# Order of splits, turns and taps on three engines, products of constants at the start, and a fourth split buffer for eight tiles, in a two-layer trunk on one core

## The reference

```python
h = rms_norm(x, norm_mix_g[i])
x = x + token_mixing(h, ...)       # w_in, conv, pool, attention, w_branch, gates, w_out
h = rms_norm(x, norm_ffn_g[i])
x = x + (swiglu(h, ...) if i % 2 == 0 else moe_ffn(h, ...))
h = rms_norm(x, norm_ple_g[i])
x = x + sigmoid(h @ ple_w_gate[i]) * (p[i] @ ple_w_proj[i])
# token_mixing, the convolution branch:
v = c_gate * u                     # three taps per channel over v, then
y_conv = b_gate * conv3(v)
```

## Time and profile before

| what | value |
|---|---|
| median of 3 runs | 1243.52 us (1242.11 to 1243.96) |
| profiled execution | 1242.05 us |
| its span, first to last instruction | 1240.3 us |
| mean granted clock of TensorE in it | 0.992 |

### The profile page before, as it was taken

The page is one execution under the profiler, slowest core; times in us unless marked ns, Lnnn a source line. Parts: engine busy times, 40 slices in busy tenths (PEclk is TensorE's granted clock), DMA queues, the critical chain, the costliest instruction groups (busy, mean ns, idle before and its releaser), DMA issues.

```text
span 1240.3 us, 15364 instructions
## 1 busy us (share of the span) xinstructions
PE 1211.2 (98%) x5976; PEld 1008.3 (81%) x5976; DVE 901.6 (73%) x864; ACT 721.5 (58%) x677; POOL 112.7 (9%) x131
## 2 busy tenths in 40 slices
PE   8999999999999999999999999999999999999997
PEld 6887787788888887897778878888888888888876
DVE  6767755654444467657766578898898988888996
ACT  5446544534343456335643467878777777777765
POOL 4700000200000010340000000001000001000301
PEclk9999999999999999999999899999999999999999
DMA  9945454656565555555445489999999999999970
GB/s 294 320 145 195 136 177 162 230 178 200 174 202 175 199 161 186 165 201 170 136 165 174 153 274 376 364 388 375 388 378 387 388 382 385 384 387 379 392 281 35
DMA packets 152204, 317.55 MB, mean 256 GB/s; under 512 B 6273, under 2 KB 41345, under 8 KB 152146
## 3 DMA queue, kind: packets, MB, share of 16 engines
q1 hardware_dynamic: 147328, 302.27, 69.6%
q0 software_dynamic: 4112, 13.44, 3.0%
q10 hardware_dynamic: 706, 1.07, 0.3%
HBM read 310.99 MB, written 5.77 MB: 255 GB/s over the span
## 4 chain that ended last, share of the span: by engine, by line
PE 82%; DVE 9%; ACT 5%; issue 3%; DMA 1%; SPq 0%; POOL 0%; POOLq 0%; ACTq 0%; DVEq 0%
PE ps L1783 22%; PE ps L1528 15%; PE ps L1529 14%; PE ps L1530 14%; PE ps L1770 11%; DVE split L961 3%; ACT split L615 3%; DMA raw<-w_in_dram 1%; PE ps L1750 1%; PE ps L1618 1%; DVE M L1336 1%; DVE hT L993 1%; PE ps L1544 1%; PE ps L1644 1%; PE ps L1739 1%
## 5 line engine op out<-in xcount | busy, mean ns | idle before, releaser
L961 DVE TENSOR_TENSOR split<-raw,split 128x2048 fp32r<-128x2048 f32 x281 | 644.6, 2298 | 242.2 <-ACT split L615 240.0
L615 ACT ACTIVATE split<-raw 128x2048 fp32r<-128x2048 f32 x281 | 538.2, 1916 | 264.2 <-PE ps L1530 190.4
L1783 PE MATMUL ps<-split,br 128*128 128x512 f32 x1344 | 317.5, 392 | 1.5 <-DVE br L1083 1.0
L1783 PEld LDWEIGHTS ps<-split,br 128*128 128x128 f32 x1344 | 249.4, 188 | 56.1 <-issue 2.0
L1528 PE MATMUL ps<-split,hT 128*128 128x512 f32 (+1 forms) x608 | 240.0, 395 | 8.4 <-DVE hT L993 3.3
L1529 PE MATMUL ps<-split,hT 128*128 128x512 f32 (+1 forms) x608 | 234.6, 386 | 0.0
L1530 PE MATMUL ps<-split,hT 128*128 128x512 f32 (+1 forms) x608 | 234.6, 386 | 0.0
L1770 PE MATMUL ps<-split,hT 128*128 128x512 f32 x672 | 159.7, 392 | 0.1
L1770 PEld LDWEIGHTS ps<-split,hT 128*128 128x128 f32 x672 | 124.8, 188 | 28.0 <-issue 1.6
L1528 PEld LDWEIGHTS ps<-split,hT 128*128 128x128 f32 x608 | 115.3, 190 | 36.1 <-DVE hT L993 5.7
L1530 PEld LDWEIGHTS ps<-split,hT 128*128 128x128 f32 x608 | 115.3, 190 | 23.1
(11 more groups left out here) (248 smaller groups left out, 934.7 us busy)
## 6 DMA issues: line engine op xcount, KB each, us to landing
raw<-moe_w_gu_dram SPq DMA_DIRECT2D x96, 1024.0 KB
raw<-moe_w_down_dram SPq DMA_DIRECT2D x56, 1024.0 KB
raw<-w_in_dram SPq DMA_DIRECT2D x45, 1024.0 KB
raw<-ffn_w_gu_dram SPq DMA_DIRECT2D x28, 1024.0 KB
raw<-moe_w_gu_dram SPq DMA_DIRECT2D x32, 512.0 KB
raw<-ffn_w_down_dram SPq DMA_DIRECT2D x14, 1024.0 KB
raw<-w_branch_dram SPq DMA_DIRECT2D x12, 1024.0 KB
raw<-w_out_dram SPq DMA_DIRECT2D x8, 1024.0 KB
```

The source lines that it names most:

```text
L615: act.activation(split[:, t % SPLIT, 0, :], raw[:, t % RAW, :], ACT.Copy).then_inc(hi, 1)
L961: dve.tensor_tensor(split[:, t % SPLIT, 1, :], raw[:, t % RAW, :], split[:, t % SPLIT, 0, :].bitcast(F32), ALU.subtract).then_inc(lo, 1)
L1783: ins = pe.matmul(ps[:, 5 if kind == "up" else 4, :], xe[:, sl, 4 * part + k, :], slot(t, sr, 512)[:, k, :], start=part + k + m == 0, stop ...
```

## The change

It does these things, all in order or place; no computation is left out.
- Constants: TensorE issues 6 products of `ones` by `ones` before it waits for the gain row, and 8 behind the two products that spread it.
- Layer one's tile 4 (second channel tile): its high part stands before the sines on ScalarE, its low part inside `angles()` between the two reductions on VectorE; tile 5's low part takes the former place of tile 4's, ahead of the rotation of k.
- Convolution, both layers: `conv_taps` makes the taps right behind the product C by u (`j in (4, 5)`), the second half into a part of `tmp`; at `j == 7` the split of tile 12 stands behind `conv_y`.
- Between the layers: `turn_lo(3)` stands before the split of u+1; the splits of u+4, u+5 and u+6 stand one place further ahead on both engines; TensorE turns block 1 inside `keys_values` of block 0, behind its sixth of eight steps.
- A fourth split buffer lies in `br` rows 0 to 3 for layer two's tiles 0 and 4, so that for its tiles 0 to 7 the high part waits for the tile four before it.

```diff
@@ -61,6 +61,8 @@
+EXTRA = 8
@@ -212,8 +214,8 @@
             "p (c n) -> p c n", c=CH)
-        cacc = M[:, 0:2, :].rearrange("p b n -> p (b n)")[:, 1536:2048].rearrange(
-            "p (c n) -> p c n", c=2)
+        cacc = [M[:, 0:2, :].rearrange("p b n -> p (b n)")[:, 1536:2048].rearrange("p (c n) -> p c n", c=2),
+                tmp[:, 512:1024].rearrange("p (c n) -> p c n", c=2)]
@@ -302,9 +304,21 @@
+        def buffer(t, s):
...
+            at = t - LAYER_T0[1]
+            if 0 <= at < EXTRA and at % (SPLIT + 1) == 0:
+                return br[:, 2 * s:2 * s + 2, :].rearrange("p r n -> p (r n)")
+            back = 0 if at < 0 else at // (SPLIT + 1) + 1 if at < EXTRA else EXTRA
+            return split[:, (t - back) % SPLIT, s, :]
...
+        def buffers(t):
...
+            return SPLIT + 1 if 0 <= t - LAYER_T0[1] < EXTRA else SPLIT
...
-            return split[:, t % SPLIT, s, :].rearrange("p (k n) -> p k n", n=n)
+            return buffer(t, s).rearrange("p (k n) -> p k n", n=n)
@@ -611,8 +625,8 @@
                 if t >= SPLIT:
-                    act.wait_ge(used, t - SPLIT + 1 + i * per)
-                act.activation(split[:, t % SPLIT, 0, :], raw[:, t % RAW, :], ACT.Copy).then_inc(hi, 1)
+                    act.wait_ge(used, t - buffers(t) + 1 + i * per)
+                act.activation(buffer(t, 0), raw[:, t % RAW, :], ACT.Copy).then_inc(hi, 1)
@@ -796,10 +810,11 @@
                 t0 = LAYER_T0[l]
-                for j in range(l, T_CHAN):
+                for j in range(l, T_CHAN if l else 2):
...
                         p_hi(0, 4)
+                        split_hi(t0 + 4)
@@ -911,6 +926,7 @@
                     p_hi(1, 6)
+                    split_hi(u + 4)
@@ -928,8 +944,6 @@
                             act.activation(sg[:, nh, :], ps[:, 2 * b + nh, :], ACT.Sigmoid).then_inc(psig, 1)
-                    if l == 0 and b:
-                        split_hi(u + 6)
@@ -940,8 +954,8 @@
                         if b == 0:
-                            split_hi(u + 4)
                             split_hi(u + 5)
+                            split_hi(u + 6)
@@ -958,8 +972,8 @@
                 dve.wait_ge(hi, t + 1 + i * per)
-                dve.tensor_tensor(split[:, t % SPLIT, 1, :], raw[:, t % RAW, :],
-                                  split[:, t % SPLIT, 0, :].bitcast(F32), ALU.subtract).then_inc(lo, 1)
+                dve.tensor_tensor(buffer(t, 1), raw[:, t % RAW, :], buffer(t, 0).bitcast(F32), ALU.subtract
+                                  ).then_inc(lo, 1)
@@ -1286,6 +1300,7 @@
                 take_off(4096 * 2 * PI, 7, 6)
+                split_lo(4)
@@ -1296,6 +1311,18 @@
+            def conv_taps(l, half):
...
+                dve.wait_ge(small_in, 48 + 96 * (l + 1))
+                dve.wait_ge(conv_v, 2 * l + half + 1)
+                for c in range(2):
+                    ch, acc = 2 * half + c, cacc[half][:, c, :]
+                    chain(dve.tensor_scalar(acc, vpad[:, ch, 0:SEQ], convw_sb[:, ch, 0:1], None, ALU.mult))
+                    for k in (1, 2):
+                        chain(dve.scalar_tensor_tensor(out=acc, in0=vpad[:, ch, k:k + SEQ],
+                                                       scalar=convw_sb[:, ch, k:k + 1], in1=acc,
+                                                       op0=ALU.mult, op1=ALU.add))
@@ -1310,7 +1337,7 @@
                            4 * l + b)
-                split_lo(t0 + 4)
+                split_lo(t0 + 4 if l else 5)
@@ -1318,28 +1345,24 @@
                 for j in range(8):
-                    split_lo(t0 + T_CHAN + j + 2)
+                    if j == 7:
+                        dve.wait_ge(conv_lo, 2 * l + 1)
+                    if 0 < j < 7 or l and j == 0:
+                        split_lo(t0 + T_CHAN + j + 2)
...
                             "p (c n) -> p c n", c=2), c_sb[:, cs, :], ALU.mult).then_inc(conv_v, 1)
+                    if j in (4, 5):
+                        conv_taps(l, j - 4)
                     if j in (6, 7):
-                        dve.wait_ge(small_in, 48 + 96 * (l + 1))
-                        dve.wait_ge(conv_v, 2 * l + j - 5)
-                        for c in range(2):
-                            ch = 2 * (j - 6) + c
-                            chain(dve.tensor_scalar(cacc[:, c, :], vpad[:, ch, 0:SEQ], convw_sb[:, ch, 0:1],
-                                                    None, ALU.mult))
-                            for k in (1, 2):
-                                chain(dve.scalar_tensor_tensor(
-                                    out=cacc[:, c, :], in0=vpad[:, ch, k:k + SEQ],
-                                    scalar=convw_sb[:, ch, k:k + 1], in1=cacc[:, c, :],
-                                    op0=ALU.mult, op1=ALU.add))
...
                         dve.tensor_tensor(ctmp, ps[:, CHAN_BANKS[j], :].rearrange("p (c n) -> p c n", c=2),
-                                          cacc, ALU.mult).then_inc(conv_y, 1)
+                                          cacc[j - 6], ALU.mult).then_inc(conv_y, 1)
+                        if j == 7:
+                            split_lo(t0 + T_CHAN + j + 2)
@@ -1479,9 +1502,8 @@
                     norm(2, 1)
+                    turn_lo(3)
                     split_lo(u + 1)
-                if l == 0:
-                    turn_lo(3)
@@ -1489,6 +1511,7 @@
                     p_lo(1, 6)
+                    split_lo(u + 4)
@@ -1515,10 +1538,8 @@
                         if b == 0:
-                            split_lo(u + 4)
+                            split_lo(u + 5)
                         turn_lo(4, (2 * b, 2 * b + 1))
-                        if b == 0:
-                            split_lo(u + 5)
@@ -1559,10 +1580,10 @@
-            def idle_work(count, bank):
+            def idle_work(count, bank, lhs=below, rhs=ident):
                 for _ in range(count):
-                    pe.matmul(ps[:, bank, 0:P], below[:, :], ident[:, :], start=True, stop=True)
+                    pe.matmul(ps[:, bank, 0:P], lhs[:, :], rhs[:, :], start=True, stop=True)
@@ -1835,20 +1856,24 @@
-            def keys_values(t, b):
+            def keys_values(t, b, between=None):
...
                                   tile_pair(t, 256, k, slice(0, 256)), k == 0, k == KD - 1)
+                    if between and k == KD - 3:
+                        between()
...
             pe.wait_ge(consts, 1)
+            idle_work(6, 5, ones, ones)
...
                           ).then_inc(g_spread, 1)
+            idle_work(8, 5, ones, ones)
@@ -1863,8 +1888,7 @@
                         pe.wait_ge(psig, 4)
-                        keys_values(t0 + 2, 0)
-                        turn(4 * l, Y, y_of(3 * l), (2, 3))
+                        keys_values(t0 + 2, 0, lambda: turn(4, Y, y_of(3), (2, 3)))
```

## The result

The changed kernel takes 1233.62 us, the median of 4 runs (1230.22 to 1234.06), beside 1243.11 us for the kernel before (4 runs, 1242.11 to 1243.96): ratio 0.9918, 95% interval 0.9907 to 0.993, so 9.5 us faster. Its profiled execution took 1234.06 us (span 1232.2 us), 8.0 us less than the profiled one before.

What follows compares the result with a forecast made beforehand. TensorE, busy 98% of the span, bounds the kernel, so only its own stream or idle stretches count. Terms +0.5 - 3.0 - 2.3 - 5.2 = -10.0 us took the median from 1243.5 to 1233.5 us, range 1231.0 to 1237.5.

Steps and rivals of the forecast that it cites:

- Part 1: Products of constants at the beginning: gain at most 0.2 us, loss bounded at 2.5 us, taken as +0.5 us.
- cold front: Rival, chance 0.22: clock stays low through the last 8 constant products; +2.5 instead of +0.5 us, 1235.5 us.
- Part 2: Layer one's second channel tile: split moved up into the angles, TensorE's 2.91 us wait goes, -3.0 us.
- Part 3: Convolution taps, both layers: TensorE's wait for the second half's product goes twice, -2.3 us (bounds -2.0 and -2.6).
- The taps' leads: Later tiles' splits, 7 us ahead of use, hide the moved taps; without that lead, up to 2.9 us a layer.
- collision of the moved taps with GpSimd: Taps exclude GpSimd's trailing averages by the two-SBUF-input rule; single steps grow 1 or 2 us, covered by the lead.
- Part 4: From layer one to layer two: waits and a low-clock stretch go, -5.2 us together (bounds -2.2 and -5.6).
- turns first: Before the gate product at 466.48: turns' low parts ahead of a split, TensorE's 0.91 us wait goes, -0.9 us.
- splits: Before layer two's keys at 497.30: last split begins 3.1 us earlier, the 1.84 us wait goes, -1.9 us.
- clock and inner turn: Behind the keys' gap: no fall to 1.2 GHz, -1.6 us; second block's turns six products earlier, -0.8 us.
- Nothing behind is there to swallow it: After the changed stretches the gain reaches the end: TensorE is busy 60.05 of 60.10 us in the expert stretch.
- The other rivals: Late last split, 1236.6 us (0.12); VectorE sets the pace, 1242.5 us (0.03); weight stream bounds, 1249 us (0.03).

Runs made afterwards that it cites:

- the six alone: The changed kernel with the first 6 products of constants, without the 8 behind the gain row: 1232.83 us.
- first kernel above: The changed kernel without the 14 products of constants at the beginning, all else as changed: 1231.81 us, ratio 0.9905.

## Why the prediction was right, and where it was not

The median was forecast at 1233.5 us and is 1233.62; the sum, -10.0 us, is -8.0 in the profiled pair and -9.5 in the medians. The closeness is partly luck: one step failed by 2.4 us and 0.5 us was lost in the routing, other terms were mis-sized by 0.9 us the other way, and the medians differ by 1.5 us more than the profiled executions.

- **Part 1 failed.** I took +0.5 us, "near the lower end, because uninterrupted work ... should bring the higher clock before the last lot ends". It did not: TensorE worked without a gap from 1.06 us and the clock rose at 12.34, half a microsecond before that of the kernel before. The "cold front" rival was the case, with +2.9 us. Even its bound, 2.5 us, was short. The cover of 0.93 us before the first turn was there (8.63 with the six alone, behind the same idle 0.93 us), but the sum left out the 0.64 us by which the six push the gain row, which I had put at up to 0.4 and then not added: 3.6 + 0.6 - 0.9 is 3.3 us, and the first turn was 3.2 us late, the fourth piece's product 2.9. The rival's total, 1235.5 us, was not met, because of the next points. In ten traces with constants in front the clock rose before 11 us once. That the gain would be at most 0.2 us held against the kernel before: in the early case it was nil.
- **Part 2 held**: -3.1 us for -3.0. The cover of half a microsecond before the third channel tile held too: without the constants, where the late front's 2.9 us don't add to it, TensorE had no wait there either (first kernel above).
- **Part 3 was mis-sized** by 0.4 us: -2.7 for -2.3, by the traces, -2.1 by whole runs. The slower start behind a gap counts with it. The taps' leads held. A collision of the moved taps with GpSimd is hardly to be seen: one tap took 0.72 us where its twin took 0.35. It has one tensor as input, so it isn't the case of two that the prediction had; the two-input taps beside GpSimd's work kept 0.5 us each, and GpSimd's last step there took 0.96 us instead of 0.74:

```profile
62.35 0.35 DVE L1321 TENSOR_SCALAR M<-M,convw_sb 128x256 f32<-128x256 f32 x1
...
63.78 0.72 DVE L1321 TENSOR_SCALAR M<-M,convw_sb 128x256 f32<-128x256 f32 x1
```

- **Part 4 held**, -5.6 us for -5.2, and in its terms: turns first -1.2 (-0.9), splits -2.1 (-1.9), clock and inner turn -2.3 (-2.4). The last split ran from 489.82 to 492.11 and TensorE used it at 492.39, so the cover of 0.3 us was about right. The wait of 0.2 us that I left before block 1's products is there, 0.27 us. The reason that I gave for the clock, that it falls behind such a gap, had a case against it in the same trace, which I passed over: no fall behind the 2.91 us before the second channel tile. So that term came out right, but why the clock fell behind one gap and not behind the other stays open.
- **"Nothing behind is there to swallow it"** missed 0.5 us in the routing, where TensorE waits for VectorE's chain of small steps.
- The other rivals did not come: no wait was given back a tile later, and the weight stream kept its pace. That the order, not VectorE's load, sets the pace is shown by each part undone: its own wait came back in its trace, with the fall of the clock behind it where parts 2 and 4 were undone, and no other wait grew by as much as 0.5 us.

The version without the 14 products has the lowest medians: 1231.81 and 1232.73 us on two chips, 1.8 and 1.9 us under the changed kernel's. The traces show why (the marks up to the second layer's scores stand 2.6 us earlier in one and 1.4 or 1.5 in the other, whose clock rose at 15.79); by whole runs alone it would not be shown, since the difference is within the 2.5 us that the prediction called no difference, the intervals overlap, and the fastest single run of all, 1230.22 us, has the constants.

## What to carry to other kernels

Work that is put in only to keep a clock up has to fit under its cover at the *low* clock; if it stands in front of a serial chain, what sticks out of the cover is paid in just the runs in which it was to help. When an operation that waits for a buffer is moved ahead, list what is queued behind it: here the additional buffer was the condition for the order. And a change made of several parts should be undone part by part, each with a trace: here one part in four cost 2.9 us of the 11.4 that the others brought.

## What the runs showed of the hardware

When TensorE's clock rises at the start is not set by the program alone: with the same instructions up to that point it rose at 4.69, 11.63, 12.34, 13.0 and 13.8 us in different traces, and with the constants left out at 12.8 to 15.8 us. Where 16 records stand before the first turn this moves the turn by 3.1 us (8.08 to 11.20). The stretch at half clock in the routing was 10.24 us long in some traces and 13.65 in others, for the same instructions; two traces of the changed kernel, one of each, agree to 0.02 us up to the second layer's scores and differ by 0.7 us at the first expert. Comparisons of a microsecond or two between such kernels need the marks of a trace beside the medians: the taps were 0 us by one median and 2.7 us by the trace of the same kernel.
